# A second block problem in the last gate/up group of both networks, and one partial sum formed a step earlier

## The reference, cut to what matters

```python
def swiglu(x, w_gate, w_up, w_down):
    return (jax.nn.silu(x @ w_gate) * (x @ w_up)) @ w_down
...
x = x + 0.5 * swiglu(rms_norm(x, ffn1_norm[l]), ffn1_w_gate[l], ffn1_w_up[l], ffn1_w_down[l])
...
x = x + 0.5 * swiglu(rms_norm(x, ffn2_norm[l]), ffn2_w_gate[l], ffn2_w_up[l], ffn2_w_down[l])
```

## Time and profile before

| | us |
|---|---|
| median of three runs | 1760.78 (1760.4 to 1761.28) |
| profiled execution, its own time | 1760.41 |
| its span, first to last instruction | 1758.6 |
| PE busy in the span | 1747.8 |
| DVE busy | 1521.5 |
| ACT busy | 1055.9 |
| mean granted TensorE clock | 0.998 of full speed |

### The profile page before, as it was taken

One profiled execution on the slowest core, in us unless ns is written; L12 is line 12 of the kernel. 1 busy time (PEld: TensorE's weight loads), 2 busy tenths in 40 slices (PEclk: granted clock), 3 DMA queues, 4 the chain that ended last, 5 costly groups with the idle time before them and its releaser, 6 DMA issues.

```text
span 1758.6 us, 21446 instructions
## 1 busy us (share of the span) xinstructions
PE 1747.8 (99%) x7791; PEld 1440.0 (82%) x7791; DVE 1521.5 (87%) x1760; ACT 1055.9 (60%) x1262; POOL 297.7 (17%) x581
## 2 busy tenths in 40 slices
PE   9999999999999999999999999999999999999998
PEld 7888888888888888888888888888888888888886
DVE  7799999999887786777878888899999999887786
ACT  7566666666555554555555456566666666555544
POOL 0102111111112112111121131121111111210001
PEclk9999999999999999999999999999999999999999
DMA  7756666666676667657555667666666666676654
GB/s 268 239 204 213 206 216 221 228 221 214 206 238 216 213 193 239 204 170 223 191 183 169 212 216 253 221 209 205 218 224 227 222 219 214 210 252 208 221 191 133
DMA packets 201802, 374.92 MB, mean 213 GB/s; under 512 B 19808, under 2 KB 20448, under 8 KB 201696
## 3 DMA queue, kind: packets, MB, share of 16 engines
q1 hardware_dynamic: 182992, 351.97, 59.8%
q0 software_dynamic: 18272, 21.01, 4.1%
q10 hardware_dynamic: 432, 0.56, 0.1%
HBM read 351.44 MB, written 4.19 MB: 202 GB/s over the span
## 4 chain that ended last, share of the span: by engine, by line
PE 99%; DMA 0%; SPq 0%; ACT 0%; DVE 0%; issue 0%; DVEq 0%; ACTq 0%
PE bank L905 17%; PE bank L907 17%; PE bank L908 17%; PE bank L922 10%; PE bank L923 10%; PE bank L924 10%; PE bank L1043 4%; PE bank L1046 4%; PE bank L1045 4%; PE bank L887 1%; PE bank L888 1%; PE bank L889 1%; DMA x<-in_x_dram 0%; PE bank L1231 0%; PE bank L1248 0%; PE bank L1104 0%
## 5 line engine op out<-in xcount | busy, mean ns | idle before, releaser
L1326 ACT ACTIVATE w_hi<-raw 128x1024 fp32r<-128x1024 f32 x443 | 467.3, 1058 | 309.8 <-PE bank L908 199.1
L1787 DVE TENSOR_TENSOR w_lo<-raw,w_hi 128x1024 fp32r<-128x1024 f32 x443 | 540.1, 1224 | 127.9 <-ACT w_hi L1326 123.0
L2647 POOL DMA_DIRECT2D turn_in<-gate x448 | 219.1, 497 | 837.0 <-DVE gate L1897 762.1
L905 PE MATMUL bank<-w_hi,xT_hi 128*128 128x512 f32 x812 | 318.1, 392 | 0.0
L907 PE MATMUL bank<-w_lo,xT_hi 128*128 128x512 f32 x812 | 316.1, 389 | 0.0
L908 PE MATMUL bank<-w_hi,xT_lo 128*128 128x512 f32 x812 | 316.1, 389 | 0.0
L905 PE MATMUL bank<-w_hi,hT_hi 128*128 128x512 f32 x528 | 205.4, 389 | 0.0
L907 PE MATMUL bank<-w_lo,hT_hi 128*128 128x512 f32 x528 | 205.4, 389 | 0.0
L908 PE MATMUL bank<-w_hi,hT_lo 128*128 128x512 f32 x528 | 205.4, 389 | 0.0
L1340 ACT ACTIVATE w_hi<-first_b 128x1024 fp32r<-128x1024 f32 x140 | 148.7, 1062 | 90.7 <-PE bank L908 38.2
L1340 ACT ACTIVATE w_hi<-second_b 128x1024 fp32r<-128x1024 f32 x129 | 136.9, 1061 | 104.7 <-DVE second_b L2064 47.3
(11 more groups left out here) (259 smaller groups left out, 2884.0 us busy)
## 6 DMA issues: line engine op xcount, KB each, us to landing
raw<-in_ffn_w_down_dram SPq DMA_DIRECT2D x132, 512.0 KB, 4.8
raw<-in_ffn_w_up_dram SPq DMA_DIRECT2D x102, 512.0 KB, 6.3
raw<-in_ffn_w_gate_dram SPq DMA_DIRECT2D x101, 512.0 KB, 5.8
raw<-in_w_in_dram SPq DMA_DIRECT2D x80, 512.0 KB, 4.3
first_b<-in_ffn_w_gate_dram SPq DMA_DIRECT2D x40, 512.0 KB, 4.1
first_b<-in_ffn_w_up_dram SPq DMA_DIRECT2D x40, 512.0 KB, 4.5
second_b<-in_ffn_w_gate_dram SPq DMA_DIRECT2D x34, 512.0 KB, 5.3
second_b<-in_ffn_w_up_dram SPq DMA_DIRECT2D x34, 512.0 KB, 5.4
```

The costliest lines, as they stand in the source:

```text
L905: pe.matmul(acc, hi[:, kt, ts], w_hi[slot][:, kk], start=(opens and kk == 0), stop=False, skip_group_check=problems(ffn, c) > 0)
L1326: act.activation(w_hi[f % RING][:], raw[m % RING][:], ACT.Copy).then_inc(hi_ready, 1)
L1787: dve.tensor_tensor(w_lo[f % RING][:], src[:], w_hi[f % RING][:].bitcast(F32), ALU.subtract)\
L2647: pool.dma_start(to[32 * j:32 * j + 32, q].rearrange("r k t i -> r (k t i)"), mid[32 * q:32 * q + 32, j].rearrange("r k t i -> r (k t i)") ...
```

## The change

Both networks' round 10 gets two block problems instead of one; rounds 9 and 10 thereby follow the patterns (2, 2) and (2, 1) where they were (2, 1) and (1, 1). The list for (2, 1) is rewritten. Since the second problem of round 10 uses `second_s_lo` to its end, the split of group 8's hidden values moves behind it, and the block b11 of that problem lies in `kept_down`. The down projection's blocks `second_b12` and `second_b22` wait for round 10's second problem. Other steps of rounds 9 and 10 get other places. In every round with two problems now and two in the next, `second_sum(0)` moves from behind P3 q1 to behind P3 q0.

```diff
@@ -72,7 +72,7 @@
 OUT_ORDER = [4, 5, 6, 7, 0, 1, 2, 3]
 
 
-PROBLEMS = ((0, 1, 2, 2, 2, 2, 2, 2, 2, 2, 1, 1, 2), (0, 2, 2, 2, 2, 2, 2, 2, 2, 2, 1, 1, 2))
+PROBLEMS = ((0, 1, 2, 2, 2, 2, 2, 2, 2, 2, 2, 1, 2), (0, 2, 2, 2, 2, 2, 2, 2, 2, 2, 2, 1, 2))
 ROUNDS = GROUPS + XG // 2
 FIRST, LAST = GROUPS, GROUPS + 1
 G, U, P1, P2, P3, P4, P5, P6, P7 = "G", "U", "P1", "P2", "P3", "P4", "P5", "P6", "P7"
@@ -84,7 +84,7 @@
 LATE_AFTER = {(0, FIRST): (6, 9, 11, 12, 13, 14, 15), (0, LAST): (6, 8, 10, 11, 12, 13, 14),
               (1, FIRST): (6, 9, 11, 12, 13, 14, 15), (1, LAST): (5, 7, 9, 10, 11, 12, 12)}
 MORE_AFTER = {(1, LAST): (1, 3, 5, 6, 7, 8, 9)}
-CHAIN_AFTER = {(2, 2): (0, 0, 0, 0, 1, 1, 1, 1, 2, 2), (2, 1): (0, 0, 1, 1, 2), (1, 1): (0, 1, 2, 3, 4),
+CHAIN_AFTER = {(2, 2): (0, 0, 0, 0, 1, 1, 1, 1, 2, 2), (2, 1): (0, 1, 2, 2, 3), (1, 1): (0, 1, 2, 3, 4),
                (0, 2): (1, 1, 2, 2, 3, 3, 4, 4, 5, 5), (0, 1): (1, 2, 3, 4, 5), (1, 2): (0, 0, 1, 1, 2, 2, 3, 3, 4, 4)}
 LAST_AFTER = (6, 6, 8, 8, 10, 10, 12, 12, 14, 14)
 REST_AFTER = {2: (0, 1, 2, 2), 1: (0, 2)}
@@ -406,6 +406,8 @@
         mid, turned_in = in_quads(gate), in_quads(turn_in)
 
         def blocks(c):
+            if c == FIRST - 1:
+                return (first_b11, kept_down), (first_b12, second_b12), (first_b22, second_b22)
             if c < FIRST:
                 return (first_b11, second_b11), (first_b12, second_b12), (first_b22, second_b22)
             if c == FIRST:
@@ -601,8 +603,9 @@
 
 
                     if c == FIRST:
-                        sp.wait_ge(lo_ready, ch + AT[ffn, c - 2, P4, 1] + 1)
-                        sp.wait_ge(chunk_used, ch + AT[ffn, c - 2, P7, 1] + 1)
+                        sp.wait_ge(chunk_used, ch + AT[ffn, c - 1, P7, 1] + 1)
+                        if p == P4:
+                            sp.wait_ge(lo_ready, ch + AT[ffn, c - 1, P4, 1] + 1)
                     elif c == LAST:
                         sp.wait_ge(chunk_used, ch + AT[ffn, FIRST, G, 0])
                         if q == 0:
@@ -1536,7 +1539,7 @@
                         continue
                     if c == 1 and n == 1 and at == (0, U, 1):
                         split_tokens(1, 1, 2 * ffn + 1)
-                    if c == GROUPS - 1 and at == (1, P1, 0):
+                    if c == GROUPS - 1 and at == (0, U, 1):
                         split_tokens(FIRST, 0, token_use(ffn, FIRST, 0) + 1)
                     if c == FIRST:
                         if at == (0, G, 12):
@@ -1582,7 +1585,7 @@
                             keep_up_lower()
                         if at == (1, P6, 1):
                             open_gate_upper()
-                        if at == (0, U, 2):
+                        if at == ((1, P2, 0) if c == GROUPS - 2 else (0, U, 2)):
                             split_hidden(hid_of(ffn), c - 1)
                         if at == (1, P7, 0):
                             keep_up_upper()
@@ -1596,13 +1599,15 @@
                             keep_up_lower()
                         if at == (1, P6, 0):
                             open_gate_upper()
+                        if at == (0, U, 3):
+                            split_hidden(hid_of(ffn), c - 1)
                         if at == (1, P7, 0):
                             keep_up_upper()
+                        if at == (1, G, 0):
+                            open_gate_lower()
                         if at == (1, P2, 0):
-                            split_hidden(hid_of(ffn), c - 1)
-                            open_gate_lower()
-                        if at == (1, G, 2):
                             gated(0)
+                        if at == (1, G, 1):
                             gated(1)
                     elif m == 2:
                         if at == (1, P3, 1):
@@ -2153,10 +2158,10 @@
                         low(ch + AT[ffn, g, kind, k], form_in(g, kind, k))
                     if kind is None and k == RING - 1 and ffn == 0:
                         add_squares(q0 + 3)
-                    if c == GROUPS - 1 and at == (0, G, 5):
+                    if c == GROUPS - 1 and at == (0, U, 0):
                         token_blocks(FIRST, 0, ch, ffn)
                         token_sum(FIRST, 0, token_use(ffn, FIRST, 0))
-                    if c == GROUPS - 1 and at == (0, U, 1):
+                    if c == GROUPS - 1 and at == (1, P5, 0):
                         split_tokens(FIRST, 0, token_use(ffn, FIRST, 0))
                     if c == FIRST:
                         if at == (0, G, 3):
@@ -2329,23 +2334,25 @@
                                 turn_lower()
                             if at == (1, P1, 1):
                                 first_sum(1)
+                            if at == (1, P3, 0):
+                                second_sum(0)
                             if at == (1, P3, 1):
-                                second_sum(0)
                                 second_sum(1)
                             if at == (1, P6, 1):
                                 third_sum(0)
                             if at == (0, U, 2):
                                 third_sum(1)
-                            if at == (0, U, 3):
+                            if at == (0, U, 3) and c < GROUPS - 2:
                                 split_hidden(hid, c - 1)
                         else:
+                            if at == (0, G, 3):
+                                turn_lower()
                             if at == (1, P1, 0):
                                 first_sum(0)
-                                turn_lower()
                             if at == (1, P3, 0):
                                 second_sum(0)
+                            if at == (1, P6, 0):
                                 third_sum(0)
-                            if at == (1, P2, 0):
                                 split_hidden(hid, c - 1)
                     if n == 1:
                         if at == (0, G, 3):
@@ -2374,6 +2381,9 @@
                     if m == 2:
                         if at == (1, G, 1):
                             fourth_sum(nx, 0)
+                            if c == GROUPS - 2:
+                                dve.wait_ge(chunk_used, ch + AT[ffn, nx, P7, 1] + 1)
+                                split_hidden(hid, c - 1)
                         if at == (1, P2, 1):
                             up_sums(c)
                     if m == 1 and at == (1, G, 2):
```

## The result

| | before | after |
|---|---|---|
| median | 1760.72 (6 runs, 1760.4 to 1761.28) | 1769.64 (6 runs, 1767.36 to 1771.12) |
| profiled execution | 1760.41, span 1758.6 | 1767.49, span 1765.6 |

The ratio is 1.005, with a 95% interval of 1.0039 to 1.0061: the change made the kernel slower. A second set of five runs of the changed kernel gave 1768.59 (1767.03 to 1770.95).

A forecast was written before the change was run, and what follows sets the result against it. PE was taken to bound the kernel, with DVE 97% busy in a (2, 2) round. On 1760.41 us: -2.72 + 0.3 + 0.3 + 2 x 2.97 + 2 x 0.96 = +5.74, 1766.2 us; range 1761.0 to 1769.5.

The forecast's parts named there:

- the two large waits: Round 10: PE waits for DVE's low parts up to U3, 2.97 us a network, and for P7's bank copy, 0.96.
- the transfers: Round 10: U1's chunk, issued behind second_b12, has eight microseconds to land before DVE needs it; no cost.
- Matmuls removed: One more problem a network takes 42 matmuls in place of 48: 12 fewer at 0.227 us, -2.72 us.
- the second sum moved: Rounds with two problems now and next: q1's sum comes 0.02 us later, nothing or +0.3 us over 15 waits.
- the wait at U2: PE's wait for U2's low part in (2, 2) rounds: 0.15 us each, 17 times; two new ones cost +0.3 us.
- 131 ns a matmul: The skill's rate for 512 columns would make the matmuls' gain 1.57 us; set aside for the measured 227 ns.
- DVE through round 10: DVE's chain from P4 q1 makes U3's low part late: 2.97 us a network, bounds 0.4 and 3.0.
- the rival's 420.65: When P3's low part is ready if DVE has no backlog; with the copy bare 1761.0 us, no change, chance 0.14.
- The copy behind P7: Round 11's first G chunk waits for ACT's copy of P7's bank, no longer covered by U5: 0.96 us a network.
- slower than I count: Rival: each DVE instruction holds the next until its end, 1.5 us a network more, 1769.2 us; chance 0.09 for 1768 to 1771.
- side remark, a transfer late into U1: A transfer coming late into U1 or P2 would end in the same place as slower DVE steps, 1768 to 1771 us.

The follow-up runs named there:

- Experiments 11: Kernel before, last U chunk's low part of round 10 (U5) computed five times instead of once: 1766.47 us; seven times: 1775.4 us.
- 12: Changed kernel with third sum early, hidden values' split late, and U3's low part of round 10 computed three times: 1771.56 us.
- experiment 2: Kernel before with only second_sum(0) moved behind P3 q0 in rounds with two problems now and next: 1760.81 us, ratio 1.0002.
- experiment 6: Changed kernel; in round 10 DVE's third sum right behind the second, the split of hidden values behind U3's low part: 1764.11 us.
- Experiment 3: Changed kernel with SP issuing U1's chunk of round 10 ahead of the blocks second_b12 and second_b22: 1767.67 us.
- Experiments 4: Changed kernel without DVE's four token-sum instructions in round 10, output not the reference's: 1769.54 us.
- 5: Changed kernel with U1's chunk issued ahead of the two blocks and round 10's four token-sum instructions left out: 1764.03 us.
- experiments 7: Changed kernel with P7 ahead of round 10's last U chunk and the split of hidden values behind that chunk's low part: 1766.02 us.
- 9: Changed kernel, three reorderings: U1's chunk issued earlier, ACT's bank copy before round 9's gate activation, third sum early with split late: 1762.51 us, ratio 1.0011.
- Experiment 8: Changed kernel with ACT's copy of P7's bank ahead of the gate's activation at the end of round 9: 1770.41 us.

## Why the prediction was wrong

The direction and the two large waits held, the size did not. The forecast was +5.7 on the profiled execution, where +7.1 was measured; by the medians it is +8.9, and 1769.64 lies just above the range's end of 1769.5. The profiled execution (1767.49) and the second set's median (1768.59) lie inside: which side of 1769.5 a median falls on depends on how many of its executions had a stretch at half clock. Three terms were put at nothing and were not: the clock, the transfers ("Nothing waits") and the first G chunk of round 10. The first is the step that put the median out of the range.

*The clock*: the forecast has no sentence on it. The waits alone give 1767.4 to 1767.8, inside the range. Each stretch at half clock adds 1.6, and most runs have one or two. Experiments 11 and 12 show the wait to be the cause. That one execution with a 2.1 us wait has it and the next has not goes with the time of the wait counted from the clock's first rise (table above). The Trainium skill ("TensorE: Matmul & The Clock Gate", What's actually happening) says that the gate looks at TensorE's activity in a rhythm of its own that does not start with the kernel; by that the same wait would meet it in some executions and not in others, and the table agrees.

*Matmuls removed* and *the second sum moved*: right, by the count of PE's rows and by experiment 2; the wait at U2 stands in all 17 rounds, 0.02 us longer ahead of its start, as forecast. The 131 ns a matmul of the Trainium skill ("TensorE: Matmul & The Clock Gate", Back-to-back issue gap) do not hold for these matmuls of 512 columns: their starts lie 227 ns apart in every profile, at the full clock.

*DVE through round 10*: right as a mechanism (experiment 6), 0.3 to 0.4 us a network too small. The step that failed in it is "Nothing waits" on the transfers. U1's chunk, issued behind the two blocks, took 6.7 us to land, and DVE came to U1 within 0.1 us of its high part, so it was no wait of DVE's; but ACT had three instructions queued behind the landing. I had asked when DVE turns to the chunk, not when ACT does. Experiment 3 takes the 0.66 us gap away and 0.8 us a network with it, and what is left, 2.50 in its network 2, is 0.47 less than the forecast's 2.97: the missing transfer and chain terms that were too long in part cancelled, which is luck. Experiments 4 and 5 show that the landing alone was enough to hold PE, and that DVE's load could not be seen until the landing was out of the way. One slip in the working changes nothing: the rival's 420.65 is 420.57 by its own terms.

*The copy behind P7*: forecast 0.96, measured 1.01; right (experiments 7 and 9).

*No term at all* stood for the first G chunk of round 10, 0.38 a network: ACT's split of the hidden values now stands ahead of G1's high part and the activation of the gate, and the copy that PE waits for comes behind them. Experiment 8 shows the copy's place in that line to be the cause, and the loss to be free here: without it PE loses as much at P1.

Of the rivals, "slower than I count" ended nearest to the time (1769.2), but by its side remark, a transfer late into U1, and not by its mechanism: steps of 1.14 us stayed 1.14.
